# Turning the state-space products of a hybrid decoder kernel and splitting its output projection by groups, on one Trainium2 core

## The reference, cut to what matters

```
xbc = silu(causal_depthwise_conv(xbc, conv_w, conv_b))
xs, bm, cm = split(xbc)                       # xs: 16 heads of 64; bm, cm: 2 groups of 128 states
m_mat = (cm . bm) * segsum_exp(dt * a_neg)    # per head: keys x queries
y = m_mat applied to xs*dt, + d_skip * xs     # [256, 1024]
y = y * silu(z)
y = rmsnorm(y.reshape(256, 2 groups, 512), ssm_norm)
x = x + concatenate([attn, y], axis=-1) @ w_out     # attn 512 wide, y 1024 wide
```

## Time and profile before

| | |
|---|---|
| median of 3 runs | 1420.45 us (1420.17 to 1420.66) |
| the profiled execution: its own time / its span | 1420.29 us / 1418.5 us |
| TensorE (PE) busy | 1409.1 us (99%) |
| weight loads of TensorE (PEld) busy | 1199.3 us (85%) |
| VectorE (DVE) busy | 992.0 us (70%) |
| ScalarE (ACT) busy | 835.6 us (59%) |
| GpSimd (POOL) busy | 80.2 us (6%) |
| mean granted clock of TensorE | 0.998 |

### The profile page before, as it was taken

One profiled execution on the slowest core, in us unless ns is written; L12 is line 12 of the kernel. 1 busy time (PEld: TensorE's weight loads), 2 busy tenths in 40 slices (PEclk: granted clock), 3 DMA queues, 4 the chain that ended last, 5 costly groups with the idle time before them and its releaser, 6 DMA issues.

```text
span 1418.5 us, 20958 instructions
## 1 busy us (share of the span) xinstructions
PE 1409.1 (99%) x8226; PEld 1199.3 (85%) x8226; DVE 992.0 (70%) x1366; ACT 835.6 (59%) x1337; POOL 80.2 (6%) x86
## 2 busy tenths in 40 slices
PE   9999999999999999999999999999999999999998
PEld 8887888888888878888888888888888888888886
DVE  5698766676567987666666788676666788666665
ACT  7775555544567654555555788455545788555553
POOL 0113200000002220000000000000000000000001
PEclk9999999999999999999999999999999999999999
DMA  8754456666376445476664525567653634556661
GB/s 287 226 151 125 156 164 196 199 198 194 111 227 178 149 135 163 152 218 199 190 192 141 175 89 164 179 193 219 192 185 107 221 104 141 177 187 194 196 190 59
DMA packets 174513, 245.52 MB, mean 173 GB/s; under 512 B 18880, under 2 KB 117840, under 8 KB 174416
## 3 DMA queue, kind: packets, MB, share of 16 engines
q1 hardware_dynamic: 174224, 244.11, 55.1%
q10 hardware_dynamic: 192, 0.08, 0.0%
HBM read 243.10 MB, written 1.05 MB: 172 GB/s over the span
## 4 chain that ended last, share of the span: by engine, by line
PE 98%; DVE 1%; DMA 0%; POOL 0%; ACT 0%; issue 0%; POOLq 0%; SPq 0%; ACTq 0%
PE misc L932 21%; PE acc L570 19%; PE acc L576 19%; PE acc L573 19%; PE misc L940 11%; PE misc L664 3%; PE misc L706 1%; PE misc L672 1%; PE misc L731 1%; PE misc L883 1%; PE misc L884 1%; PE misc L881 0%; PE misc L685 0%; DVE w_lo L1482 0%; PE misc L785 0%; DMA w_raw<-in_w_in 0%
## 5 line engine op out<-in xcount | busy, mean ns | idle before, releaser
L1482 DVE TENSOR_TENSOR w_lo<-w_raw,w_hi 128x1024 fp32r<-128x1024 f32 (+2 forms) x466 | 550.8, 1204 | 219.6 <-ACT w_hi L1062 218.1
L1062 ACT ACTIVATE w_hi<-w_raw 128x1024 fp32r<-128x1024 f32 (+2 forms) x466 | 473.1, 1039 | 243.0 <-PE misc L940 107.2
L932 PE MATMUL misc<-h_both,w_hi 128*128 128x512 f32 x1280 | 312.9, 391 | 0.0
L932 PEld LDWEIGHTS misc<-h_both,w_hi 128*128 128x128 f32 x1280 | 235.0, 188 | 45.3
L570 PE MATMUL acc<-w_hi,h_both 128*128 128x512 f32 (+2 forms) x768 | 206.9, 390 | 0.3 <-ACT h_both L1101 0.3
L576 PE MATMUL acc<-w_hi,h_both 128*128 128x512 f32 (+2 forms) x768 | 198.8, 380 | 0.9 <-DVE h_both L1523 0.9
L573 PE MATMUL acc<-w_lo,h_both 128*128 128x512 f32 (+2 forms) x768 | 198.8, 380 | 0.0
L940 PEld LDWEIGHTS misc<-h_both,w_lo 128*128 128x128 f32 x1280 | 164.1, 191 | 6.3
L940 PE MATMUL misc<-h_both,w_lo 128*128 128x256 f32 x1280 | 166.0, 283 | 0.0
L576 PEld LDWEIGHTS acc<-w_hi,h_both 128*128 128x128 f32 x768 | 140.7, 188 | 28.9 <-DVE h_both L1523 2.1
L573 PEld LDWEIGHTS acc<-w_lo,h_both 128*128 128x128 f32 x768 | 140.8, 188 | 27.7 <-DVE w_lo L1482 0.2
(11 more groups left out here) (237 smaller groups left out, 1178.5 us busy)
## 6 DMA issues: line engine op xcount, KB each, us to landing
w_raw<-in_w_in SPq DMA_DIRECT2D x112, 512.0 KB, 4.6
w_raw<-in_w_gate SPq DMA_DIRECT2D x176, 256.0 KB, 3.1
w_raw<-in_w_up SPq DMA_DIRECT2D x176, 256.0 KB, 3.7
w_raw<-in_w_down SPq DMA_DIRECT2D x88, 512.0 KB, 4.1
w_raw<-in_w_out SPq DMA_DIRECT2D x40, 512.0 KB, 3.5
w_raw<-in_w_in SPq DMA_DIRECT2D x16, 336.0 KB, 4.4
w_raw<-in_w_proj_a SPq DMA_DIRECT2D x8, 512.0 KB, 4.1
w_raw<-in_w_proj_b SPq DMA_DIRECT2D x8, 512.0 KB, 3.9
```

The source lines that it names most:

```text
L932: mm = pe.matmul(bank[:, :], w_hi[:, r, cols], h_both[:, tile, :, :].rearrange("p u t -> p (u t)"), start=tile == 0, stop=tile == KD - 1)
L1062: act.activation(w_hi[:, g % RING, 0:w], w_raw[:, g % RING, 0:w], ACT.Copy)\
L1482: dve.tensor_tensor(w_lo[:, g % RING, 0:w], w_raw[:, g % RING, 0:w], w_hi[:, g % RING, 0:w].bitcast(F32), ALU.subtract)\
```

## The change

In both layers of the second block:

- **Products turned.** `y0` to `y7` become `Y0` to `Y3`, one for two pairs of heads. The 128x64 tile of `xs` of a head is now stationary and `E` moves: 256 columns for the first tile of keys, 128 for the second. The two heads of a pair write the lower and the upper 64 partitions. The result `ysT` has channels on the partitions. `pairs_out` adds `d_skip` times the turned `cv`.
- **Gate turned.** `zT0` to `zT3` transpose z (16 transposes) in the place of `ssT0` to `ssT3`. z0 goes through silu before it is transposed, as it did; z1 is transposed raw and gets a Tanh and `(tanh + 1) * z` with the half folded into the gains.
- **Norm.** ScalarE squares the turned tiles whole (`gated_rows`), and TensorE sums them over channels: `ms0` and `ms1`, for each group eight float32 products with a 128x128 stationary tile of squares and 2 moving columns. The gains become per-partition scalars. The factor is no longer applied to y, but to the product.
- **Output projection in three parts.** `wo0` and `wo1` accumulate two slots at a time (attention, group 0, group 1). After each part VectorE adds it into `x` (`group_residual`), for the groups times their factor; the next part of the same half waits for that.
- **Places and order.** `Ex` has four places for pairs of heads, the operand halves are made from `ysT` in SBUF (`h_hi`, `h_lo`), two more pads stand behind `O4`, and `split_until` has new bounds in both lists.

```diff
-        PT0 PT1 S2 S3 xb1 O0 xT0 xT1 xb1 xb2 PT2 PT3 S4 S5 xb2 O2 xT2 xT3 xb2 xb2 PT4 PT5 z0 O4 pad0 xT4 xT5
+        PT0 PT1 S2 S3 xb1 O0 xT0 xT1 xb1 xb2 PT2 PT3 S4 S5 xb2 O2 xT2 xT3 xb2 xb2 PT4 PT5 z0 O4 pad0 pad1 pad2 xT4 xT5
         z0 cs z0 z0 xsT0 xsT2 xsT1 xsT3 cr0 cr1 z1 cb0 cb1
-        z1 y0 cr2 cr3 z1 y1 z1 y2 cr4 cr5 wo0 y3 wo0 y4 cr6 cr7 wo1 y5 wo1 ssT0 ssT1 y6 y7 wo0 wo0 wo1
-        ssT2 ssT3 wo1 wo0 wo0 wo1 mT0 mT1 wo1 mT2 mT3"""
+        z1 cr2 cr3 z1 Y0 z1 zT0 cr4 cr5 zT1 wo0 Y1 wo0 cr6 cr7 wo1 Y2 wo1 zT2 zT3 wo0 ms0 Y3 wo0 wo1 wo1
+        wo0 ms1 wo0 wo1 mT0 mT1 wo1 mT2 mT3"""
...
+                part = 2 if c.stat == "mix" else len(c.slots)
+                if i and i % part == 0:
+                    pe.wait_ge(*DV_.at(layer, f"{name}.s{i // part - 1}"))
...
+                elif kind == "Y":
+                    pe.wait_ge(*DV_.at(layer, f"M{2 * i + 1}"))
...
+                    for half in range(2):
+                        hp = 2 * i + half
+                        for keys in range(NT):
+                            for u in range(2):
+                                cols = slice((2 * hp + u) * SP, (2 * hp + u + 1) * SP)
+                                mm = pe.matmul(b[64 * u:64 * u + 64, half * T + keys * P:(half + 1) * T], xs[:, keys, cols],
+                                               Ex[hp % 4][:, u, 2 * keys * P:(2 + keys) * P],
+                                               start=keys == 0, stop=keys == 1)
...
+                elif kind == "ms":
+                    pe.wait_ge(*AC.at(layer, f"sq{2 * i + 1}"))
+                    b = bank_of(layer, name)
+                    for t in range(NT):
+                        for k in range(4):
+                            mm = pe.matmul(b[:, 2 * t:2 * t + 2], sqs[:, 4 * i + k, t * P:(t + 1) * P], halves[:, 0:2],
+                                           start=k == 0, stop=k == 3)
...
+                def group_residual(i, n, names):
+                    end = ORD[1].slot_no[f"wo{i}", 2 * n + 1]
+                    if n == 2:
+                        split_until(layer, end + 1 + LOOK)
+                    dve.wait_ge(*PE.of("used", BASE[layer] + end))
...
+                        dve.scalar_tensor_tensor(out=v, in0=acc[2 * ORD[1].pair[f"wo{i}"] + t][:, :],
+                                                 scalar=small[:, c:c + 1], in1=v, op0=ALU.mult, op1=ALU.add)\
+                            .then_inc(*DV_.mark(name))
...
+                split_until(layer, z + 13)
+                group_residual(1, 1, ["wo1.s1", "wo1.s1"])
+                split_until(layer, z + 14)
+                group_rows(1)
                 for i in range(2):
-                    banks = wait_product(layer, f"wo{i}")
-                    residual(layer, [(i, t, banks[t]) for t in range(NT)], [f"wo{i}.t{t}" for t in range(NT)])
+                    group_residual(i, 2, [f"wo{i}.t{t}" for t in range(NT)])
                     norm_operand(layer, f"mT{2 * i}")
                     norm_operand(layer, f"mT{2 * i + 1}")
```

More of the change, by code:

```diff
@@ L275 @@
      **{f"yT{i}": ("h", 2 * i, 2, 0.5) for i in range(4)}},
-    {**{f"ssT{i}": ("h", 2 * i, 2, 1.0) for i in range(4)}},
+    {},
 )
@@ L281 @@
      ("pb0", 0): "hgT1", **{("wo0", i): f"yT{i}" for i in range(4)}},
-    {**{("q", i): f"nT{i}" for i in range(4)}, ("wo0", 0): "O4", ("wo0", 2): "ssT1",
-     ("wo0", 4): "ssT3"},
+    {**{("q", i): f"nT{i}" for i in range(4)}, ("wo0", 0): "O4", ("wo0", 2): "ss3",
+     ("wo0", 4): "ss7"},
 )
@@ L489, in params @@
                 else:
-                    sp.dma_start(gains[:, G_SSM:G_SSM + SI], row("ssm_norm_2", l, SI)).then_inc(par_in, 16)
+                    sp.dma_start(rows[60:68, :], A["ssm_norm_2"][l:l + 1, :].rearrange("a (k p) -> (a k) p", p=P))\
+                        .then_inc(par_in, 16)
                     for i, name in enumerate(("dt_bias_2", "a_log_2", "d_skip_2")):
@@ L2044, in body_b @@
-                for hp in range(SH // 2):
-                    weighted_decays(hp)
-                    if hp == 0:
-                        split_until(layer, ORD[1].before["misc", "cr1"] + 3)
-                    if 1 <= hp < SH // 2 - 1:
-                        head_pair_out(hp - 1)
-                    if hp % 2 and hp < SH // 2 - 1:
-                        exponents(hp + 1)
-                        exponents(hp + 2)
-                        split_until(layer, ORD[1].before["misc", f"cr{hp + 1}"] + (3 if hp == 1 else LOOK))
-                    if hp == 4:
-                        times_silu(0)
-                    if hp == 5:
-                        normalised(0)
@@ L2058, in body_b @@
-                operand(layer, "ssT0")
-                operand(layer, "ssT1")
-                head_pair_out(SH // 2 - 2)
-                head_pair_out(SH // 2 - 1)
-                times_silu(1)
-                normalised(1)
-                operand(layer, "ssT2")
-                operand(layer, "ssT3")
+                z = ORD[1].before["misc", "cr1"]
+                weighted_decays(0)
+                split_until(layer, z + 3)
+                weighted_decays(1)
+                exponents(2)
@@ new lines, in body_b @@
+                exponents(6)
+                exponents(7)
+                low_rows(0)
+                split_until(layer, z + 8)
+                group_residual(0, 0, ["wo0.s0", "wo0.s0"])
+                weighted_decays(6)
+                low_rows(1)
+                split_until(layer, z + 9)
+                weighted_decays(7)
+                pairs_out(2)
+                split_until(layer, z + 10)
+                group_residual(1, 0, ["wo1.s0", "wo1.s0"])
+                turned_gate(2)
```

192 lines of the change are left out of this document (121 added, 71 removed).

## The result

| | before | after |
|---|---|---|
| median | 1420.43 us (1420.17 to 1420.75, 6 runs) | 1426.09 us (1425.57 to 1426.20, 6 runs) |
| the profiled execution: own time / span | 1420.29 / 1418.5 us | 1426.15 / 1424.4 us |
| TensorE (PE) / its weight loads (PEld) busy | 1409.1 / 1199.3 us | 1409.0 / 1193.4 us |
| VectorE (DVE) / ScalarE (ACT) busy | 992.0 / 835.6 us | 1001.7 / 837.0 us |

The change makes the kernel slower: the ratio is 1.0039, 95% interval 1.0028 to 1.0050, or +5.7 us. TensorE's busy time has hardly moved, and its idle time has grown by what the span has.

What follows compares the result with a forecast made beforehand. TensorE, busy 99% of the span, was taken as the bound. Work of -0.3 and waits of 1.45, 0.45 and 1.65 made +3.25 us a layer, +6.5 in two: 1420.3 + 6.5 = 1426.8 us, range 1421.5 to 1432.5.

Steps and rivals of the forecast that it cites:

- out: `y0` to `y7` with edges: TensorE work removed: eight steps of 1.25 us, three longer sweeps behind and small waits, 10.5 us less a layer.
- in: `Y0` to `Y3` with edges: TensorE work added: four turned steps of 1.44 us, some 1.6 with edges, 6.5 us a layer, pairs overlapping.
- in: `ms0`, `ms1` with edges: TensorE work added: sixteen small float32 products at 0.22 us each, 3.6 us a layer with edges.
- other (edges, transposes, `cr`), the remainder: Moved TensorE work: sixteen transposes and four `cr` steps unchanged, one more edge, +0.1 us a layer.
- wait at `xT4`: Behind `O4`: with three pads `xT4` writes `O4`'s bank and waits for its readers, +1.45 us a layer.
- wait at `cr2`: `cr2` and `cr3` write the banks of `cr0` and `cr1` and wait for ScalarE's read, +0.45 us a layer.
- wait at `mT0`: `mT0` waits for `wo0`'s last addition, behind the reading of `ms1` and five low halves on VectorE, +1.65 us a layer.
- At nothing: Terms costed at zero: VectorE's growth to about 55 of 64 us, ScalarE's table load before the feed-forward's first Silu.
- VectorE as the bound: Rival: low halves come late, +2.2 to 2.6 us a layer, up to 1431 to 1432 us; chance 0.18.
- no overlap: Rival: turned pairs in `Y` don't overlap, 11.2 instead of 6.5, +4.7 us a layer, 1436 us; chance 0.03.
- Nearly free small products: Rival: `ms0` and `ms1` cost next to nothing instead of 3.5 us a layer, 1419.8 us, no change; chance 0.06.
- rival 1: The rival VectorE as the bound, chance 0.18; its sum with half as much again was given as 1434 us.

Runs made afterwards that it cites:

- experiment 1: The changed kernel with the two new pads moved from behind `O4` to just ahead of `cr2`: 1421.63 us.
- experiment 2: The kernel before with one wait added, `xT4` waiting for VectorE's low half of `O4`: 1423.34 us.
- experiment 3: The changed kernel with two instead of five low halves ahead of the last addition of `wo0` on VectorE: 1424.94 us.
- experiment 9: The spread version with four needless 128x512 additions on VectorE in each layer, in `wo0`'s part: 1420.94 us.
- spread version: The changed kernel with the new pads moved to ahead of `cr2` and the feed-forward weights' low halves spread over VectorE's idle time: 1418.22 us.
- experiment 8: The spread version with two needless 128x512 additions on VectorE in each layer, in `wo0`'s part: 1418.54 us.
- 10 to 12: The spread version with `Y`'s inner loops exchanged, 1418.95 us; all products of one half first, 1423.71; both heads' stationary tile at whole width, 1426.28.
- experiment 7: The spread version with 64 instead of 2 moving columns in each small summing product: 1418.46 us.

## Why the prediction was right

Forecast 1426.8 us, measured 1426.09, with the sign, the mechanism and three places as given. By its steps, a layer:

| step | predicted | measured |
|---|---|---|
| out: `y0` to `y7` with edges | -10.5 | -10.79 |
| in: `Y0` to `Y3` with edges | +6.5 | +6.58 |
| in: `ms0`, `ms1` with edges | +3.6 | +3.57 |
| other (edges, transposes, `cr`), the remainder | +0.1 | -0.35 |
| wait at `xT4` (`O4` to `cr0`) | +1.45 | +1.66 |
| wait at `cr2` | +0.45 | +0.41 |
| wait at `mT0` | +1.65 | +1.69 |
| sum, a layer | +3.25 | +2.77 |

- **Out.** In the trace of before, from start to start, the eight steps took 10.33 us. The sweeps behind four of them were 0.09 to 0.10 longer, and 0.09 passed ahead of `y4`. The prediction took three such sweeps and 1.25 for each step, where `y0` and `y4` took 1.36.
- **In.** Four `Y` at 1.45, 0.09 to 0.10 ahead of three of them and 0.12 to 0.13 more in the sweep behind each: 6.58. `ms` took 1.78 and 1.70 with 0.1 behind the second: 3.6. Both prices were read from rows of the same form (`O2`, `cs`), and both were right to 0.1 us.
- **Other, the term that was mis-sized.** It was put at one more edge, +0.1, and the remainder is -0.35. The last `cr` step now takes 0.46 us instead of 0.56, and the sixteen transposes with their edges are some 0.05 cheaper. The three slots between a `cr` and a `y` took 2.79, 2.78 and 2.78 us before, where a plain one takes 2.72; now such slots lose some 0.1 less in all. The last 0.1 is spread over rows and not assigned. Together with "out" and "in" this makes the work 0.99 us a layer shorter instead of 0.3, which is 1.4 us of the program. Waits that were larger by 0.2 a layer, and the 0.3 that stood ahead of the first `O4`, took back half of it. That the forecast missed by only 0.7 is in part luck of this kind.
- **Waits.** `xT4` came out 0.2 larger. ScalarE, held by a high half until 830.99, read `O4` 1.66 us behind `O4`'s start instead of 1.54, and TensorE started 0.14 behind VectorE's end (831.47 + 0.43 = 831.90, then 832.04), for which the prediction had 0.04. `cr2` and `mT0` were right to 0.05, `cr2` by two errors that cancel: ScalarE ended only 0.27 us behind TensorE's arrival instead of 0.42 (851.34 + 0.62 = 851.96 against 851.69), and the 0.14 until TensorE starts was not counted. Experiments 1 and 2 show the wait at `xT4` by its removal and by adding it alone, experiment 1 the one at `cr2` (together with `xT4`'s), experiment 3 the one at `mT0`.
- **At nothing.** VectorE's growth stayed covered: no sweep waits for a low half in the changed kernel, and the slack measured in experiment 9 on the spread version is within the band that was read. VectorE's busy time grew by 9.7 us, 4.85 a layer, where the prediction's terms give 16.5 - 11.8 + 0.6 = 5.3. ScalarE's table load for the feed-forward harms nothing:

```profile
918.29 0.84 ACT L1169 ACTIVATE arena<-acc,small 128x256 f32<-128x256 f32 x2 [1.77 <-PE acc L581]
```

ScalarE has stood idle for 1.77 us, the load behind it, before the last sweep lets this Silu start. In the earlier trace rows VectorE's product stood with 4.3 us to spare, and the load takes none of that.
- **The rivals.** VectorE as the bound fell with experiments 8 and 9, no overlap with 10 to 12. Nearly free small products fell with the 1.8 us of `ms` and with experiment 7. The Trainium skill (TensorEngine Tiling (Array Packing), Instruction Overhead) puts a matmul at about 60 cycles, and the estimate by it was 1421.4. The 0.11 us a piece in the rows stand against it. One sum of rival 1 is off, and nothing rests on it: with half as much again, 5.25 less 0.9 to 1.3 a layer, it comes to about 1435 and not 1434.

The stretch from `cr0` to `wo1`'s end, for which the prediction named 62.6 us, ends where the next slot starts: 842.39 to 903.22 before, 60.83 us, and 844.37 to 906.32 after, 61.95. It is 0.65 shorter than named, which is the work that was mis-sized (0.99 instead of 0.3). To `mT2`, one slot on, it is 64.67 against 63.56.

## What to carry to other kernels

A step that writes a rotating bank waits for whoever read it last, so removing or merging steps, or adding a pad, can put a wait in front of a step that the change does not touch; go through the turns again after every change of the order. Where an engine works through a list and makes things ahead of time, put them where it stands idle, and not in a lump in front of what the bound engine wants next; here, moving the lump moved three quarters of the wait with it. Here the version with turned products and both places mended takes 1418.22 us against 1420.39 for the kernel before, and 1415.88 with rounded squares.

## What the runs showed of the hardware that was not expected

- Overlap on the two 64-column halves does not need partners side by side: 1.45 us with alternating products, 1.51 with two of a half in a row, 2.15 with four, 2.53 at whole width. Going into the 64-column form cost 0.10 us ahead of a step, which is gone at whole width.
- A product with hardly any moving columns was not cheap here, with a 128x128 stationary tile: 0.11 us a piece with 2 as with 64 columns, and the same 0.11 for an fp32r piece (0.87 us for eight). Fewer pieces did save (0.9 us for eight less).
- A wait moved is not a wait removed: of 1.69 us at `mT0`, 1.26 came back at `mT2` once the first was gone.
